# Decoder trunk: pre-norm weights applied to the transposed x, transposes taken from h itself, and a reordered start of the rotary products

## What is computed

```python
def rmsnorm(x, g):
    y = x * lax.rsqrt(jnp.mean(x * x, axis=-1, keepdims=True) + NORM_EPS)
    return y * g

for i in range(DEPTH):                      # DEPTH = 2
    f = swiglu(rmsnorm(h, ffn1_pre_g[i]), ffn1_w_in[i], ffn1_w_down[i])
    h = h + 0.5 * rmsnorm(f, ffn1_post_g[i])
    hn = rmsnorm(h, mix_pre_g[i])
    mixed = hybrid(hn) if i % 2 == 0 else mla_attention(hn)
    h = h + rmsnorm(mixed, mix_post_g[i])
    f = swiglu(rmsnorm(h, ffn2_pre_g[i]), ffn2_w_in[i], ffn2_w_down[i])
    h = h + 0.5 * rmsnorm(f, ffn2_post_g[i])
    gate = jax.nn.sigmoid(rmsnorm(h, ple_pre_g[i]) @ ple_w_gate[i])
    h = h + rmsnorm(gate * (p[i] @ ple_w_proj[i]), ple_post_g[i])
```

## Time and profile before

| | |
|---|---|
| Median of 3 runs | 1106.6 us (1106.44 to 1106.68) |
| Profiled execution: its time | 1107.31 us |
| Profiled execution: span of its instructions | 1104.7 us |
| PE busy | 1096.1 us, 99% of the span |
| DVE busy | 815.0 us, 74% |
| ACT busy | 568.8 us, 51% |
| POOL busy | 83.5 us, 8% |
| Granted TensorE clock | full in all 40 slices |
| DMA | 208.35 MB, mean 189 GB/s |

### The profile page before, as it was taken

How to read it: one execution, slowest core, us unless ns; L and a number is a source line. 1 busy time by engine, 2 the same in 40 slices (tenths; PEclk the granted TensorE clock), 3 DMA queues, 4 the chain that set the end, 5 groups by cost and what they waited for, 6 DMA issues and landing times.

```text
span 1104.7 us, 14117 instructions
## 1 busy us (share of the span) xinstructions
PE 1096.1 (99%) x5716; PEld 933.7 (85%) x5716; DVE 815.0 (74%) x1078; ACT 568.8 (51%) x703; POOL 83.5 (8%) x138
## 2 busy tenths in 40 slices
PE   9999999999999999999999999999999999999997
PEld 6888888888888888888888888888898888888886
DVE  5787777588997677667776867767876667776785
ACT  7534434568464554444565544346785555444443
POOL 3200000201110200000013000001200020000011
PEclk9999999999999999999999999999999999999999
DMA  8755555645544555555556555554533365555551
GB/s 338 241 190 191 190 191 186 251 171 188 191 172 152 210 219 191 190 190 191 184 196 214 214 190 191 190 190 158 224 115 99 104 242 188 192 190 194 190 175 57
DMA packets 31599, 208.35 MB, mean 189 GB/s; under 512 B 3760, under 2 KB 3808, under 8 KB 8112
## 3 DMA queue, kind: packets, MB, share of 16 engines
q1 hardware_dynamic: 27792, 193.48, 49.1%
q0 software_dynamic: 3600, 13.46, 3.5%
q10 hardware_dynamic: 144, 0.52, 0.1%
HBM read 206.39 MB, written 1.06 MB: 188 GB/s over the span
## 4 chain that ended last, share of the span: by engine, by line
PE 95%; DVE 2%; issue 1%; DMA 1%; ACT 0%; POOL 0%; POOLq 0%; DVEq 0%
PE PS L771 24%; PE PS L186 17%; PE PS L188 17%; PE PS L187 17%; PE PS L768 12%; PE PS L383 1%; PE PS L2000 1%; DMA raw<-stream 1%; DVE WL L168 1%; PE PS L2021 1%; PE PS L1286 1%; PE PS L2002 1%; PE PS L2011 0%; PE PS L1273 0%; PE PS L1292 0%
## 5 line engine op out<-in xcount | busy, mean ns | idle before, releaser
L168 DVE TENSOR_TENSOR WL<-raw,WH 128x2048 fp32r<-128x2048 f32 x180 | 411.3, 2290 | 160.5 <-ACT WH L161 160.4
L161 ACT ACTIVATE WH<-raw 128x2048 fp32r<-128x2048 f32 x180 | 342.8, 1908 | 84.0 <-DMA raw<-stream 83.7
L771 PE MATMUL PS<-X,WH 128*128 128x512 f32 x1152 | 276.0, 391 | 0.0
L771 PEld LDWEIGHTS PS<-X,WH 128*128 128x128 f32 x1152 | 213.1, 188 | 42.2
L874 ACT ACTIVATE sgb<-sgb 128x256 f32<-128x256 f32 x72 | 30.0, 417 | 262.3 <-DVE sgb L870 262.3
L768 PEld LDWEIGHTS PS<-X,WL 128*128 128x128 f32 x1152 | 143.5, 192 | 3.1
L768 PE MATMUL PS<-X,WL 128*128 128x256 f32 x1152 | 144.5, 283 | 0.0
L186 PE MATMUL PS<-WH,X 128*128 128x512 f32 (+2 forms) x356 | 138.9, 390 | 0.0
L188 PE MATMUL PS<-WL,X 128*128 128x512 f32 (+2 forms) x356 | 136.7, 384 | 0.0
L187 PE MATMUL PS<-WH,X 128*128 128x512 f32 (+2 forms) x356 | 136.6, 384 | 0.0
L186 PE MATMUL PS<-WH,BH 128*128 128x512 f32 x288 | 113.2, 393 | 0.0
(11 more groups left out here) (291 smaller groups left out, 1319.1 us busy)
## 6 DMA issues: line engine op xcount, KB each, us to landing
raw<-stream SPq DMA_DIRECT2D x181, 1024.0 KB, 4.8
PG<-post_g POOLq DMA_DIRECT2D x8, 512.0 KB, 6.7
QG<-pre_g POOLq DMA_DIRECT2D x7, 512.0 KB, 7.4
Eg<-acs_rows POOLq DMA_DIRECT2D x2, 1024.0 KB, 7.3
raw<-stream SPq DMA_DIRECT2D x3, 512.0 KB, 7.0
h<-x SPq DMA_DIRECT2D x4, 256.0 KB, 5.3
out<-h SPq DMA_DIRECT2D x4, 256.0 KB, 2.0
raw<-stream ACTq DMA_DIRECT2D x1, 512.0 KB, 4.5
```

The costliest lines, as they stand in the source:

```text
L161: act.activation(WH[:, n % RING, :], raw[:, n % RING, :], ACT.Copy).then_inc(sem("w_hi"), 1)
L168: dve.tensor_tensor(WL[:, n % RING, :], raw[:, n % RING, :], WH[:, n % RING, :], ALU.subtract).then_inc(sem("w_lo"), 1)
L771: ins = pe.matmul(PS[:, bank, :], wh[:, kt, cols], X[:, kt, :, :].rearrange("p a n -> p (a n)"), start=opens, stop=closes, skip_group_chec ...
```

## The change

Three things are changed.

First, the multiplication `normed` goes, with `hn_done` and the row `QG`. PE transposes h itself, and waits for `h_new`. The pre-norm weights of all eight stages are loaded once, by one small DMA from POOL's queue, as columns (`pre_cols`, 128 by 64), and `x_high` and `x_low` multiply by a column on the way out of PSUM. Each therefore takes four instructions of 128 columns for a half instead of one of 512.

Second, some transposes move one product earlier: those of the first tile wherever `wide` calls `middle` (now ahead of its second and third product), which holds for the ends of ffn, hyb and mla and for the second tile in ple, and the second tile's first half in mla and in an ffn that does not follow ple. The second tile in hyb and the transposes around the change from ple to ffn stay where they were.

Third, in mla the rotation is cut in two, and the first tile's two first products stand ahead of the second tile's `latents_low`.

```diff
             for c in range(2):
                 for q in range(2):
-                    if c and middle is not None:
-                        middle(q)
+                    if (c, q) in ((0, 1), (1, 0)) and middle is not None:
+                        middle(c)
...
             for b in range(2):
                 update_h(dve, s, t, b)
-                if s + 1 < NS:
-                    normed(dve, s + 1, t, b)
-        def normed(dve, s, t, b):
-            h_ready(dve, s, t, b)
-            if (t, b) == (0, 0):
-                dve.wait_ge(sem("qg"), 16 * s)
-            dve.tensor_tensor(hn[:, t, half(b)], h[:, t, half(b)], QG[:, half(b)], ALU.mult)\
-               .then_inc(sem("hn_done"), 1)
...
             for a_ in halves:
                 if s:
-                    pe.wait_ge(sem("hn_done"), 4 * (s - 1) + 2 * t + a_ + 1)
+                    h_ready(pe, s, t, a_)
...
-                                       (hn if s else h)[:, t, kt * P:(kt + 1) * P], ident[:, :])
+                                       h[:, t, kt * P:(kt + 1) * P], ident[:, :])
...
+        def x_gain(s, kt):
+            return pre_cols[:, s * KT + kt:s * KT + kt + 1]
...
                 act.wait_ge(sem("x_tr"), 4 * s + 2 * t + a_ + 1)
-                act.activation(x_half(XH, t, a_), x_psum(s, t, a_), ACT.Copy).then_inc(sem("x_hi"), 1)
+                for q in range(4):
+                    kt = 4 * a_ + q
+                    ins = act.activation(XH[:, kt, tok(t)], PS[:, x_bank(s, t, a_), q * P:(q + 1) * P], ACT.Copy,
+                                         scale=x_gain(s, kt))
+                ins.then_inc(sem("x_hi"), 1)
...
                 dve.wait_ge(sem("x_hi"), 4 * s + 2 * t + a_ + 1)
-                dve.tensor_tensor(x_half(XL, t, a_), x_psum(s, t, a_), x_half(XH, t, a_), ALU.subtract)\
-                   .then_inc(sem("x_lo"), 1)
+                for q in range(4):
+                    kt = 4 * a_ + q
+                    ins = dve.scalar_tensor_tensor(XL[:, kt, tok(t)], PS[:, x_bank(s, t, a_), q * P:(q + 1) * P],
+                                                   x_gain(s, kt), XH[:, kt, tok(t)], ALU.mult, ALU.subtract)
+                ins.then_inc(sem("x_lo"), 1)
...
-            if s + 1 < NS:
-                if s:
-                    pool.wait_ge(sem("hn_done"), 4 * s)
-                pool.dma_start(QG[:, :], a["pre_g"][s + 1, :].partition_broadcast(P)).then_inc(sem("qg"), 16)
+            if not s:
+                pool.dma_start(pre_cols[:, :], a["pre_g"]).then_inc(sem("pre_cols"), 16)
...
-                    if s and (j, t, q) == (lead, 0, 2):
+                    if s and (j, t, q) == (lead, 0, 2 if lead > 2 else 1):
                         transpose_x(pe, s, 1, (0,))
...
-                    if (j, t, q) == (1, 0, 2):
+                    if (j, t, q) == (1, 0, 1):
                         transpose_x(pe, s, 1, (0,))
...
+            turn_begin(0)
             latents_low(1)
             split_to(u + 4)
-            turn(0)
-            turn(1)
+            turn_finish(0)
+            turn_begin(1)
+            turn_finish(1)
```

More of the change, by code:

```diff
@@ L87, in hybrid_trunk @@
         PG = place("PG", [P, D])
-        QG = place("QG", [P, D])
+        pre_cols = place("pre_cols", [P, NS * KT])
         hn_at = at[0]
@@ L133, in sem @@
             return sems[name]
-        for name in ("raw0", "raw1", "raw2", "raw3", "raw4", "w_hi", "w_lo", "w_used", "x_in00", "x_in01", "x_in10", "x_in11", "zeros", "consts", "pg", "qg", "qg_cols", "w_part0", "w_part1", "w_part2", "w_part3", "x_piece", "x_lo_piece", "w_part_hi", "w_lo_half",
-                     "out_done", "ple_done", "post_sq", "post_ms", "post_y", "post_rs", "h_new", "pre_sq", "pre_rs", "hn_done",
+        for name in ("raw0", "raw1", "raw2", "raw3", "raw4", "w_hi", "w_lo", "w_used", "x_in00", "x_in01", "x_in10", "x_in11", "zeros", "consts", "pg", "pre_cols", "qg_cols", "w_part0", "w_part1", "w_part2", "w_part3", "x_piece", "x_lo_piece", "w_part_hi", "w_lo_half",
+                     "out_done", "ple_done", "post_sq", "post_ms", "post_y", "post_rs", "h_new", "pre_sq", "pre_rs",
                      "x_tr", "x_hi", "x_lo", "gate", "silu", "up", "acted", "h_tr", "h_hi", "h_lo",
@@ L398, in x_half @@
             return tile[:, 4 * a_:4 * a_ + 4, tok(t)]
-        def x_psum(s, t, a_):
-            return PS[:, x_bank(s, t, a_), :].rearrange("p (k n) -> p k n", n=P)
+        def x_gain(s, kt):
+            return pre_cols[:, s * KT + kt:s * KT + kt + 1]
         def x_high(act, s, t, halves=(0, 1)):
+            if s == 1:
+                act.wait_ge(sem("pre_cols"), 16)
             for a_ in halves:
                 act.wait_ge(sem("x_tr"), 4 * s + 2 * t + a_ + 1)
-                act.activation(x_half(XH, t, a_), x_psum(s, t, a_), ACT.Copy).then_inc(sem("x_hi"), 1)
+                for q in range(4):
[3 more added lines that the diff above has]
+                ins.then_inc(sem("x_hi"), 1)
         def x_low(dve, s, t, halves=(0, 1)):
+            if s == 1:
+                dve.wait_ge(sem("pre_cols"), 16)
             for a_ in halves:
                 dve.wait_ge(sem("x_hi"), 4 * s + 2 * t + a_ + 1)
-                dve.tensor_tensor(x_half(XL, t, a_), x_psum(s, t, a_), x_half(XH, t, a_), ALU.subtract)\
-                   .then_inc(sem("x_lo"), 1)
+                for q in range(4):
[3 more added lines that the diff above has]
+                ins.then_inc(sem("x_lo"), 1)
         def first_x_high(act, t, a_, quarters=range(4)):
@@ L2193, in mla_dve, with rotate @@
             u = first[s]
-            def rotate(x, y, t, n, tmp):
+            def rotate(x, y, t, n, tmp, begin=True, finish=True):
                 c = cosT[:, t, :].unsqueeze(1).broadcast_to([P, n, HALF])
@@ L2204, in rotate @@
                 x0, x1, y0, y1 = x[:, :, :, 0, :], x[:, :, :, 1, :], y[:, :, :, 0, :], y[:, :, :, 1, :]
-                dve.tensor_tensor(w, x0, c, ALU.mult)
-                dve.tensor_tensor(x_, x1, sn, ALU.mult)
+                if begin:
+                    dve.tensor_tensor(w, x0, c, ALU.mult)
+                    dve.tensor_tensor(x_, x1, sn, ALU.mult)
+                if not finish:
+                    return
                 dve.tensor_tensor(y_, x1, c, ALU.mult)
@@ L2232, in latents_low, with turn_begin @@
                                   cTH[:, :, tok(t)], ALU.subtract).then_inc(sem("ml_clo"), 1)
-            def turn(t):
+            def turn_begin(t):
                 n = (ROPE0, ROPE1)[t]
@@ L2238, in turn, with turn_finish @@
                 rotate(piece_view(n).rearrange("p b (n a h) -> p b n a h", a=2, h=HALF),
-                       qr[:, t, :].rearrange("p (b n a h) -> p b n a h", b=2, a=2, h=HALF), t, HEADS, tmp)\
+                       qr[:, t, :].rearrange("p (b n a h) -> p b n a h", b=2, a=2, h=HALF), t, HEADS, tmp, finish=False)
+            def turn_finish(t):
+                n = (ROPE0, ROPE1)[t]
+                rotate(piece_view(n).rearrange("p b (n a h) -> p b n a h", a=2, h=HALF),
+                       qr[:, t, :].rearrange("p (b n a h) -> p b n a h", b=2, a=2, h=HALF), t, HEADS, tmp, begin=False)\
                     .then_inc(sem("ml_qr"), 1)
@@ L2601 @@
         "stream": stream_of(STAGES, w),
-        "pre_g": gains_of(STAGES, w, "pre"),
+        "pre_g": gains_of(STAGES, w, "pre").reshape(len(STAGES) * KT, P).T,
         "pre_g0": gains_of(STAGES, w, "pre")[0].reshape(KT, P).T,
```

## The result

The changed kernel takes 1113.05 us (median of 4 runs, 1112.27 to 1113.12), the kernel before 1106.52 in the same comparison (4 runs, 1106.39 to 1106.68): a ratio of 1.0052, interval 1.0039 to 1.0065. It is 6.5 us slower. Forecast were 1111.2 and a range of 1107.6 to 1113.0, so the direction was right, the size was seven tenths of the measured one (4.6 of 6.5), and the time lies 0.05 us above the range.

A forecast was written before the change was run, and what follows sets the result against it. PE, busy 99% of the span, bounds the kernel, so only its waits count. Stage-change terms 0.9 + 0.2 + 0.6 + 1.3 + 1.9 + 0.25 + 0.1 - 0.7 = +4.55 on the median 1106.6 give 1111.2 us, range 1107.6 to 1113.0.

The forecast's parts named there:

- The price of the pieces: Each half of x: four ACT pieces take 1.14 us, four DVE pieces 1.13, making the chain 0.98 us longer.
- The cheap-pieces rival: Splitting of x: pieces cost 0.5 us more a half instead of 0.98, giving 1107.9 us; chance 0.20.
- the estimate from the fixed costs in the Trainium skill: Splitting of x: per-instruction costs of 51 ns on ScalarE, 125 on VectorE add an estimated 0.53 us a half.
- ffn to ple: FFN to per-layer embedding: second tile's x 0.5 us late, plus 0.1 for loading weights; 0.6 in sum.
- attention: Change from FFN to attention: PE starts late on x in both tiles, 1.9 us in sum, the costliest change.
- the rotary part: Inside attention: rotary products fill DVE's idle 1.29 us, so two PE waits shrink by 0.4 and 0.3 us.
- the loads on POOL's queue: Embedding to FFN and elsewhere: removing the 512 KB weight loads gains nothing; no PE wait hangs on POOL's queue.
- the square: ACT's queue ahead of attention: square of the last output, ahead of x_high, starts 0.45 us later behind the moved transposes.
- ple to ffn: Embedding to FFN: transposes 0.54 us late through h, first half of x 0.76 more; 1.3 in sum.
- a rival's: Late weight splits behind the longer halves stop PE again, up to 1 us: 1112.9; chance 0.22, shared with missing rotary gain.
- ffn to hyb: FFN to hybrid: first tile 0.1 us, second tile, whose transposes are not moved, 0.8 late; 0.9 in sum.
- Just in time, but PE can no longer load the weights ahead: 0.1: FFN to hybrid, first tile: x ready at 192.68, wanted at 192.72, so only 0.1 us is lost.

## Why the prediction came out as it did

**The bound and the method held.** PE has the same work, and the time is the sum of its waits at the stage changes. Where the forecast put a wait of half a microsecond or more, there is one.

**The price of the pieces held.** 1.14 and 1.13 us a half, as in the earlier trace rows. The cheap-pieces rival needed under 0.6 extra for a half and falls, since the trace has 1.14 + 1.13 - 0.60 - 0.69 = 0.98. So does the estimate from the fixed costs in the Trainium skill (Perfetto Trace Analysis, Optimizing Scalar/DVE Operations), 0.53. The section's other remark, that breaking up instructions may let work finish sooner, is borne out by no run here. Handed on in pairs through to PE, the pieces let PE start 2.18 us behind its transposes instead of 3.12: as soon as with the wide form of before (2.18), and not sooner.

**Right in place and size:** ffn to ple (0.70 for 0.6), attention (1.93 for 1.9), the rotary part (-0.77 for -0.7), the loads on POOL's queue (nothing, and nothing). In ffn to mla the square moved as worked out: PE was 4.22 us behind before by then, 761.12 + 4.22 = 765.34, and the square started at 765.79, 0.45 later.

**Right in sum, wrong inside:** ple to ffn. Forecast were 0.54 at the transposes and 0.76 at x. The timeline of after has three waits (PE):

```profile
589.04 0.50 PE L186 MATMUL PS<-WH,X 128*128 128x512 f32 x1 [0.37 <-DVE WL L168]
...
590.97 0.66 PE L374 MATMUL PS<-ident,h 128*128 128x128 f32 x4 [0.26 <-DVE h L329]
...
594.01 0.50 PE L186 MATMUL PS<-WH,X 128*128 128x512 f32 x1 [0.58 <-DVE X L412]
```

The first was a rival's: a late weight split stops PE, 0.53 us by the starts. In the forecast it would have come on top. It did not, because h was late anyway, and the time that PE lost there it no longer lost at the transposes: these start 0.56 later than PE's delay ahead of the change would have them (590.97 - 587.81 - 2.60), where 0.54 was forecast.

**Where it failed: the sizes of the small terms.** The direction, the places and the large terms were right; the trace's sum is 1.27 above the forecast's. Of this, 0.36 is ffn to hyb. The second tile came out at 0.97 for 0.8: the chain is 3.07 us where 2.93 was worked out, since the two handovers, from the transposes' start to ACT and from ACT's end to DVE, took 0.69 and 0.11 instead of the 0.63 and 0.03 of before. The first tile came out at 0.29 for 0.1; the step that was mis-sized there is "Just in time, but PE can no longer load the weights ahead: 0.1", a price that no row gave. Its row in after:

```profile
192.97 0.50 PE L186 MATMUL PS<-WH,X 128*128 128x512 f32 x1
```

Before it was 192.72; 0.08 of the 0.25 is older, and the matmul behind it comes 0.34 later where 0.23 is usual, another 0.1. The chain is the longer one here too, 3.07 us from 189.85, so x was there at 192.92, not 192.68, and PE wanted it at 192.72 + 0.08 = 192.80. A product that misses its operand by 0.12 lost 0.29 here, not 0.1. The same step was taken for both tiles of hyb to ffn and of mla to ffn: they lost 0.22, 0.14, 0.18 and 0.16, in sum 0.36 and 0.34 for 0.2 and 0.25.

Another 0.42 lies at two places that the forecast didn't name. In hyb, PE waits around 324 for the scan's decay tiles (`Eg`); in the kernel whose pairs go through to PE, DVE's row there ends an idle time by a DMA:

```profile
319.69 3.23 DVE L1589 TENSOR_SCALAR Eg<-Eg,sm 128x128 f32<-128x128 f32 x16 [0.29 <-DMA Eg<-acs_rows]
```

All kernels made from after show 0.09 to 0.35 here, also that with wide instructions (0.19); the two made from before show none. The DMA takes 6.1 to 6.3 us from issue to landing in the former and 5.8 in before and the latter. Why it takes longer wasn't tried and stays open; the missing loads of `QG` are not the reason, since the kernel before without them has 5.8 as well. In the ffn behind ple, PE waits at 608.16 for DVE's `act_h`, which is queued behind a weight split whose unit came late from the stream:

```profile
602.66 1.92 ACT L161 ACTIVATE WH<-raw 128x2048 fp32r<-128x2048 f32 x1 [2.18 <-DMA raw<-stream]
```

It is there in after (0.22) and in the other kernels with late x at the change ahead of it (0.14 to 0.56), and zero in the kernels with wide instructions or with pairs. In after the unit's load was issued at 597.07 against 593.07 in before, as late as PE is by then (4.00), and then took 5.6 us instead of 4.7. Why it took longer stays open.

The last 0.7 us of the 6.5 lies outside the spans, in two of the four runs; no row shows it, and no mechanism of the forecast stands for it.

## What to carry to other kernels

When an operation on the way to the engine that sets the end is cut into pieces, read the chain from release to use, not the engine's busy time: DVE became 8 us freer here and the kernel 6.5 us slower. Hand pieces on as they are done, through every engine of the chain (in pairs, the loss of 5.8 us of span fell to 0.9), and look again at what stands ahead of them in the consumer's queue (here a square that waits for PE). Price "just too late" at more than the lateness: here products that barely missed their operand lost 0.14 to 0.29 us.

## What was unexpected

One late wait can pay for another: PE's 0.53 us for the weight split at 589.04 came almost wholly off later waits, so that a stage with three waits cost what was forecast for two. And the weight stream has delays of its own: in single profiled executions PE was stopped in the last ffn by a unit that came late (in the pairs kernel with x ahead of the square, without the new gate order: ACT idle 0.98 at 1053.93, PE idle at 1061.58; after had none of it):

```profile
1053.93 1.92 ACT L161 ACTIVATE WH<-raw 128x2048 fp32r<-128x2048 f32 x1 [0.98 <-DMA raw<-stream]
...
1061.58 0.50 PE L186 MATMUL PS<-WH,BH 128*128 128x512 f32 x1 [1.03 <-DVE BL L909]
```

That execution has a span of 1105.8 where the median of its runs is 1104.9. A profile that is 1 us off its median is therefore no argument about a term of that size; the starts of the same matmuls, place by place, are.
